# A fused two-block kernel on one core: the time-step product and seven modulation strips moved ahead, and the expert weights issued in another order

## What is computed

```python
sh_a, sc_a, g_a, sh_f, sc_f, g_f = split(silu(c) @ w_mod + b_mod, 6)     # modulation, 6 x 1024 columns
hx = x * (1 + sc_a) + sh_a ; hc = ctx * (1 + mod_c[1]) + mod_c[0]
xbc = silu(dwconv(h @ w_in[:, OFF_XBC:OFF_DT]))                          # 12 tiles of 128 channels
dt = softplus(h @ w_in[:, OFF_DT:OFF_K] + dt_bias)                       # 32 time steps per token
A = -exp(a_log) ; a_cs = cumsum(dt * A) per chunk of 128 tokens
states of the two context chunks, then y of the eight token chunks, in both directions
... gate, attention, out projection, layer norm, router ...
hid = silu(t @ w_gate[e]) * (t @ w_up[e]) ; out = hid @ w_down[e]        # two of 16 experts per token
```

## Time and profile before

| what | value |
|---|---|
| median of three runs | 3334.88 us |
| the profiled execution's own time | 3342.64 us |
| its span | 3340.5 us, so 2.1 us lie around it |
| mean granted TensorE clock | 0.952 |
| busy shares of the span | PE 92%, DVE 46%, ACT 23%, POOL 32% |
| the chain that ended last, by engine | PE 82%, DVE 7%, DMA 5%, issue 3% |

### The profile page before, as it was taken

One profiled execution on the slowest core, in us unless ns is written; L12 is line 12 of the kernel. 1 busy time (PEld: TensorE's weight loads), 2 busy tenths in 40 slices (PEclk: granted clock), 3 DMA queues, 4 the chain that ended last, 5 costly groups with the idle time before them and its releaser, 6 DMA issues.

```text
span 3340.5 us, 28822 instructions
## 1 busy us (share of the span) xinstructions
PE 3075.4 (92%) x10281; PEld 1540.7 (46%) x10281; DVE 1522.6 (46%) x2470; ACT 754.1 (23%) x1568; POOL 1059.2 (32%) x982
## 2 busy tenths in 40 slices
PE   8996999998999999999698995697899999999996
PEld 4553554444455554444444442366444444444442
DVE  2433782345666665222433223539113444544446
ACT  1223854411233333011111111512211000000002
POOL 0002770000567767100000001245004444555445
PEclk8997999999999999999799998798899999999998
DMA  6000432001000000210588887101003111121101
GB/s 256 19 0 0 118 91 92 26 26 51 1 1 1 1 1 1 67 38 29 172 302 298 322 334 277 45 0 38 26 0 101 38 38 38 38 70 44 38 13 57
DMA packets 132990, 259.53 MB, mean 78 GB/s; under 512 B 24776, under 2 KB 80752, under 8 KB 120688
## 3 DMA queue, kind: packets, MB, share of 16 engines
q1 hardware_dynamic: 120304, 216.60, 18.6%
q0 software_dynamic: 6768, 24.64, 2.1%
q10 hardware_dynamic: 5776, 16.46, 1.2%
HBM read 231.98 MB, written 25.70 MB: 77 GB/s over the span
## 4 chain that ended last, share of the span: by engine, by line
PE 82%; DVE 7%; DMA 5%; issue 3%; POOL 1%; ACT 1%; SPq 0%; ACTq 0%; DVEq 0%; POOLq 0%
PE ps L3053 16%; PE ps L3069 7%; PE ps L1453 7%; PE ps L493 6%; PE ps L1045 5%; PE ps L1857 5%; PE ps L1222 5%; PE ps L1241 4%; DMA ring<-in_w_up 4%; PE ps L1257 4%; PE ps L956 3%; PE ps L2820 3%; PE ps L1876 2%; PE ps L2122 2%; PE ps L900 1%
## 5 line engine op out<-in xcount | busy, mean ns | idle before, releaser
L1334 DVE TENSOR_REDUCE arena_b<-ps 128x1 f32<-128x512 f32 (+1 forms) x384 | 217.3, 600 | 144.4 <-PE ps L1222 144.1
L3018 POOL TENSOR_TENSOR arena_b<-arena_b,arena_d 128x512 f32<-128x512 f32 x132 | 165.7, 1271 | 370.2 <-DVE arena_d L3178 368.7
L3156 DVE TENSOR_TENSOR arena_d<-arena_d,ps 128x512 f32<-128x512 f32 x154 | 102.0, 686 | 388.1 <-PE ps L3053 388.1
L1857 PE MATMUL ps<-ring,arena_a 128*128 128x512 f32 x496 | 237.6, 635 | 33.8 <-issue 18.0
L1316 POOL TENSOR_TENSOR arena_b<-arena_b 128x512 f32<-128x512 f32 x182 | 224.5, 1267 | 92.4 <-ACT arena_b L1298 92.4
L1222 PE MATMUL ps<-arena_d,arena_a 64*128 64x512 f32 (+1 forms) x768 | 234.9, 534 | 3.6 <-DVE arena_b L1325 2.9
L1241 PE MATMUL ps<-arena_a,arena_d 64*128 64x512 f32 x640 | 220.0, 607 | 2.4 <-ACT arena_b L1298 1.8
L3175 DVE TENSOR_TENSOR arena_b<-arena_b,ps 128x512 f32<-128x512 f32 x264 | 174.8, 685 | 50.9 <-POOL arena_b L3018 25.5
L1857 PEld LDWEIGHTS ps<-ring,arena_a 128*128 128x128 f32 x496 | 99.7, 204 | 168.1 <-issue 149.5
L493 PE MATMUL ps<-arena_b,ring 128*128 128x512 f32 x384 | 166.9, 592 | 0.7 <-ACT arena_t L472 0.7
L1045 PE MATMUL ps<-ring,arena_b 128*128 128x512 f32 x384 | 167.4, 592 | 0.0
(11 more groups left out here) (546 smaller groups left out, 5363.6 us busy)
## 6 DMA issues: line engine op xcount, KB each, us to landing
ring<-in_w_gate SPq DMA_DIRECT2D x42, 1024.0 KB, 7.8
ring<-in_w_up SPq DMA_DIRECT2D x42, 1024.0 KB, 10.4
ring<-in_w_down SPq DMA_DIRECT2D x42, 1024.0 KB, 6.8
ring<-in_w_in SPq DMA_DIRECT2D x10, 2048.0 KB, 15.3
ring<-in_w_mod SPq DMA_DIRECT2D x32, 512.0 KB, 4.0
yslots<-arena_a ACTq DMA_DIRECT2D x31, 512.0 KB
ring<-in_w_mod SPq DMA_DIRECT2D x4, 2048.0 KB, 13.9
ring<-in_w_out SPq DMA_DIRECT2D x4, 2048.0 KB, 7.8
```

The lines of the kernel that those rows point to most:

```text
L1334: eng.tensor_reduce(mx3[j % 2][:, t, e, piece:piece + 1], ps[:, shared("s", u), 0:k1 - k0], AX.X, ALU.max).then_inc(s_mx, 1)
L1857: mm = eng.matmul(ps[:, s % 2, :], xsT[s % 2][:, k, :], sguw[s % 2][:, :, k, :], start=(k == 0), stop=(k == KT - 1))
```

## The change

It does four things.

1. The weight `wdtw` is transferred ahead of the first panel of `w_in`, to another place (`arena_d`).
2. The time steps are computed inside the convolution stage: the product ahead of channel tile 0, the sums behind tile 0, the chunk sums inside tile 1 (behind the first eight matmuls), DVE's part ahead of its convolution of tile 0, ACT's part behind its raw copy of tile 0. PSUM banks 3 to 7 take the results. `pe_turn(0)` waits also for DVE's copies.
3. Seven strips move: strips 0, 1 and 2 (`TAIL = 3`) stand behind the last channel tile's matmuls on TensorE, ahead of the wait for the convolution's end, and strips 3 to 6 stand in the context's steps, behind the parts hb = 1 and 3. The other 25 are spread over k = 0 to 23 as `EARLY + min(25, 25 * (k + 1) // 24)`: one in each part, two in the last. ACT's copies of strips 0 and 1 stand ahead of its last silu, that of strip 2 first in `act_ssd`, those of strips 3 to 7 in part 0.
4. In `sp_slots` gate and up of s+1 are issued ahead of down of s.

```diff
             eng.dma_start(cin, io["ctx"][0].rearrange("(t p) d -> p t d", p=P)).then_inc(s_xl[2], 16)
+            eng.dma_start(wdtw, w_in[:, OFF_DT:OFF_DT + 32].rearrange("(k p) n -> p k n", p=P)
+                                  ).then_inc(s_wdt, 16)
             load_panels(eng, J_XBC, J_XBC + 3)
             after(eng, "hx")
             eng.dma_start(hc_dram, hc.rearrange("p k n -> p (k n)")).then_inc(s_spill, 16)
-            eng.dma_start(wdtw, w_in[:, OFF_DT:OFF_DT + 32].rearrange("(k p) n -> p k n", p=P)
-                                  ).then_inc(s_wdt, 16)
...
+        TAIL, EARLY = 3, 7
+
         def strips_by(k):
-            return min(NSTRIP, (4 * (k + 1) + 2) // 3)
+            return EARLY + min(NSTRIP - EARLY, (NSTRIP - EARLY) * (k + 1) // 24)
...
         def pe_xbc(eng):
             after(eng, "hx")
+            pe_dt_product(eng)
             for m in range(XT):
...
+                if m == 1:
+                    eng.wait_ge(s_rawz, DTP_COPIED)
...
+                    if m == 1 and b == b0:
+                        pe_dt_cumulated(eng)
                 mm.then_inc(s_xbc, 1)
+                if m == 0:
+                    pe_dt_sums(eng)
                 if m >= 1:
                     pe_turn(eng, m - 1)
...
+            if m == 0:
+                eng.wait_ge(s_dt, 8)
...
+            eng.wait_ge(s_packT, DT_STEP + 1)
+            eng.tensor_copy(dtp, ps[:, 3:6, :].rearrange("p a n -> p (a n)")[:, 0:L + CTX]).then_inc(s_rawz, 1)
+            dch = Chain(eng, s_dt)
+            dve_dt(eng, dch)
             for m in range(XT):
+                if m == XT - 1:
+                    dve_condition(eng, 1)
...
             for m in range(XT + 1):
+                if m == XT:
+                    for i in range(TAIL - 1):
+                        act_strip(eng, i)
...
+                if m == 0:
+                    act_dt(eng)
...
+            act_strip(eng, TAIL - 1)
             skip(0, range(HEADS)).then_inc(s_t, 1)
...
-                for i in range(strips_by(k - 1), strips_by(k)):
+                for i in range(TAIL if k == 0 else strips_by(k - 1), strips_by(k)):
                     act_strip(eng, i)
...
-            after(eng, "dt")
+            eng.wait_ge(s_raw, XT)
+            for i in range(TAIL):
+                if i >= 1:
+                    pe_strip_sum(eng, i - 1)
+                pe_strip(eng, i)
+            after(eng, "xbc", "dt")
             cb(0)
             diff(0)
...
+                    if n < CT and hb % 2:
+                        i = TAIL + 2 * n + hb // 2
+                        pe_strip_sum(eng, i - 1)
+                        pe_strip(eng, i)
...
-            for s in range(NSLOT):
+
+            def first_weights(s):
                 e = eng.value_load(eidx[0:1, s:s + 1], min_val=0, max_val=NE - 1)
                 if s >= 2:
                     eng.wait_ge(gu_done, s - 1)
                 eng.dma_start(sguw[s % 2][:, 0], gate_of[e]).then_inc(gu_in[s % 2], 16)
                 eng.dma_start(sguw[s % 2][:, 1], up_of[e]).then_inc(gu_in[s % 2], 16)
+
+            first_weights(0)
+            for s in range(NSLOT):
+                if s + 1 < NSLOT:
+                    first_weights(s + 1)
+                e = eng.value_load(eidx[0:1, s:s + 1], min_val=0, max_val=NE - 1)
                 if s >= 2:
                     eng.wait_ge(dn_done, s - 1)
                 eng.dma_start(sdnw[s % 2], down_of[e]).then_inc(dn_in[s % 2], 16)
```

More of the change, by code:

```diff
@@ L478, in h_tile, with pe_dt_product @@
             return hx[:, k, t * P:(t + 1) * P] if t < LT else hc[:, k, (t - LT) * P:(t - LT + 1) * P]
+        dtp = view(arena_a, 6000, L + CTX)
+        DTP_COPIED = 6 + 6 + 1
+        flat = lambda v: v.rearrange("p t h -> p (t h)")
+        def pe_dt_product(eng):
+            eng.wait_ge(s_wdt, 16)
+            for b, src in enumerate((hx[:, :, 0:HALF], hx[:, :, HALF:L], hc)):
+                for k in range(KT):
+                    i = k % 4
+                    mm = eng.matmul(ps[32 * i:32 * i + 32, 3 + b, 0:src.shape[2]], wdtw[:, k, :], src[:, k, :],
+                                    start=(k < 4), stop=(k >= 4))
+            mm.then_inc(s_packT, 1)
@@ new lines, in pe_dt_sums, with pe_dt_cumulated @@
+        def pe_dt_sums(eng):
+            eng.wait_ge(s_rawz, DTP_COPIED)
+            for t in range(NT):
+                mm = eng.matmul(ps[:, 6, t * 32:(t + 1) * 32], dtp[:, t * P:(t + 1) * P], sel[:, :],
+                                start=True, stop=True)
+            mm.then_inc(s_packT, 1)
+        dt_fw, dt_bw, dt_gt = (ps[:, 6, i * NT * 16:(i + 1) * NT * 16] for i in range(3))
+        dt_all, dt_lt = ps[:, 7, 0:NT * 32], ps[:, 7, NT * 32:NT * 48]
+        def pe_dt_cumulated(eng):
+            eng.wait_ge(s_dt, 6)
+            a = dta
+            eng.matmul(dt_fw, m_le[:, :], a[:, :, 0:16], start=True, stop=True)
+            eng.matmul(dt_bw, m_ge[:, :], a[:, :, 16:32], start=True, stop=True)
+            eng.matmul(dt_all, ones[:, :], a, start=True, stop=True)
+            eng.matmul(dt_gt, m_gt[:, :], a[:, :, 0:16], start=True, stop=True)
+            eng.matmul(dt_lt, m_lt[:, :], a[:, :, 16:32], start=True, stop=True).then_inc(s_packT, 1)
@@ new lines, in act_dt @@
+        def act_dt(eng):
+            eng.wait_ge(s_dt, 2)
+            eng.wait_ge(s_small, NSMALLV)
+            eng.activation(flat(cdec), flat(eacs), ACT.Exp, scale=-1.0).then_inc(s_dta, 1)
+            eng.activation(wdt[:, 0, :], rowv("a_log"), ACT.Exp).then_inc(s_dta, 1)
+            eng.wait_ge(s_dta, 1)
+            eng.activation(flat(cdec), flat(cdec), ACT.Ln, bias=1.0).then_inc(s_dta, 1)
+            eng.wait_ge(s_dt, 8)
+            eng.activation(wdt[:, :, 0:16], dt_gt.rearrange("p (t h) -> p t h", h=16), ACT.Exp
+                           ).then_inc(s_dta, 1)
+            eng.activation(wdt[:, :, 16:32], dt_lt.rearrange("p (t h) -> p t h", h=16), ACT.Exp
+                           ).then_inc(s_dta, 1)
+            eng.activation(flat(cdec), dt_all, ACT.Exp).then_inc(s_dta, 1)
+            eng.activation(flat(eacs), flat(acs), ACT.Exp).then_inc(s_dta, 1)
@@ L540, in dve_conv @@
                 ins.then_inc(s_conv, 1)
+                if m == 0:
+                    eng.wait_ge(s_dta, 7)
+                    dch(eng.tensor_tensor(wdt, wdt, dts, ALU.mult))
             chained[0] = ch.n
@@ L3327, in _ @@
             pe_xbc(eng)
-            pe_dt(eng)
             pe_ssd(eng)
```

62 lines of the change are left out of this document (18 added, 44 removed).

## The result

The changed kernel takes 3297.1 us, the median of four runs (3294.16 to 3299.06), against 3334.24 us of four runs of the kernel before (3328.01 to 3335.53). The ratio is 0.9892, with a 95% interval of 0.9874 to 0.9909. The forecast was 3299 us, in a range of 3288 to 3315. The profiled execution took 3294.16 us, with a span of 3292.1 and a mean granted clock of 0.96.

What follows compares the result with a forecast made beforehand. TensorE bounds the kernel, busy 92% of the span; gains come where it waits or work leaves its full stretches. 20.6 - 9.2 + 8.5 - 1 + 17 = 35.9 us off gives 3299 us from the median, range 3288 to 3315.

Steps and rivals of the forecast that it cites:

- Time steps, removed: Between convolution and the context's states: the time steps alone fill the chain from 280.44 to 301.32, so 20.6 us go.
- Time steps, added: Convolution stage: product 4.8, sums 2.56 and chunk sums 1.8 us delay TensorE, together 9.2 us, or 12.1 without a clock's gain.
- Rival 5: Time steps stall the convolution and DVE ends the mixing parts: 8 us less gain, 3307 us; chance 0.12.
- The small transfer: Start of the convolution stage: moving it ahead of three panels lands them 0.5 to 1 us later, at cost 0.
- Strips out of the mixing: Mixing: seven parts lose a second strip, 7 x 1.34 = 9.4 us; 8.5 taken, 5 if DVE ends some parts.
- Strips in the tail: Convolution's end: three strips, 4.0 to 8 us, fit TensorE's 8.8 us of idling; cost 0, or 1 at low clock.
- Strips in the context's steps and the clock: Context's steps: four strips overrun DVE's gaps, cost 1 to 2 us, 1 taken; stretch left at 1.2 GHz.
- Rival 2: Context's steps: the clock comes up, a step falls from 2.93 to about 2.0 us, 7 us, 3291 us; chance 0.12.
- Expert weights: Late expert slots: weights issued 6.1 us earlier cover all late waits if transfers keep up; 17 of 18.8 us gained.
- Rival 1: Expert slots: transfers are the floor, so the slots give 0 to 5 us, total 3313 us; chance 0.13.
- The early excess: Slots 1 to 13: 30.3 us over 11.43 per slot, caused by DVE's six preparation pieces, stays as they are not touched.
- rival 4: Expert slots: weights, gathers and stores choke each other, the slots take 39 us more at 290 GB/s, 3355 us; chance 0.03.

Runs made afterwards that it cites:

- The experiment: Changed kernel with the time-step weight transferred behind the three panels of w_in, not ahead of them: 3305.66 us in a single execution.
- DVE's pieces moved: Changed kernel with the old weight order and DVE's six pieces of preparation behind modulate(s+2): 3293.79 us, 0.9871 to 0.9904 against the kernel before.
- DVE's pieces later: Changed kernel, new weight order kept, with DVE's six pieces of preparation behind modulate(s+2), ahead of the store: 3266.9 us, ratio 0.9792 against the kernel before.

## Why the prediction was right

The total was 2 us off, but by terms that miss in both directions. By its own steps:

**Time steps, removed: 20.6 forecast, 20.8 measured.** From the end of the convolution stage to POOL's first product lay 301.3 - 270.3 = 31.1 us, and now 286.8 - 276.5 = 10.3.

**Time steps, added: 9.2 forecast, 8.3 measured.** From TensorE's first matmul of the stage to its last tile's end it was 270.27 - 48.23 = 222.0 us and is 276.47 - 46.14 = 230.3. The product, the sums and the chunk sums are the 4.4, 2.2 and 1.6 us above (forecast 4.8, 2.56, 1.8). The cover of about 1 us for the turn held, with a wait of 0.24. The kernel with the time steps alone gained 13.1 us in its medians, for 11.4. Rival 5's first half (a stall in the convolution) did not come.

**The small transfer: 0, right.** The experiment shows that the product is what feels its place. That the stage starts 2.1 us sooner in the first profile after is not shown to be the change's: its first matmul starts between 47.1 and 48.3 us in the three profiles with the time steps in their old place, and between 45.5 and 48.4 in the nine with the product ahead and its weight ahead of the panels.

**Strips out of the mixing: 8.5 forecast, 5.6 measured at equal clock.** This term was mis-sized. The step that failed is "7 x 1.34": the two parts that the prediction measured were both without `cb`, and its price was carried over to all. From `diag` to `diag` at the full clock, five parts with two strips and no `cb` fell from 6.56 to 5.21 us, as forecast. Two parts with two strips and `cb` fell only from 7.00 to 6.49. Three parts with `cb` that had one strip already grew, two from 5.66 to 6.49 and one from 6.22 to 6.49. The last part with strips (k = 23), which has two now, and the part behind it cost 0.2 us more together. That adds up to 5.6. Part k = 0, the eighth with two strips, waits for DVE before and after and gives next to nothing. The chain before, behind the last row, has one of the parts of 5.66 us (398.00 - 392.34; L840 is `cb`):

```profile
392.34 1.04 PE ps L864 x8
393.37 0.50 PE ps L840 x4
...
398.00 1.03 PE ps L864 x8
```

The reason is DVE: the second strip had also been slack for it. Now each part with `cb` waits for DVE, 0.76 us for L759 beside the 0.51 of the `cb` matmuls (the chain after, at 394.79). The prediction named this and kept 5 us for it, but as the poorer case; DVE had 145 of 180 us and has two products more in a `cb` part (L720, 0.76 us). So the second half of rival 5 came in part. The two profiled executions hide it: they differ by 179.6 - 171.4 = 8.2 us, of which 2.8 are half of the 5.6 us that the first spent at 1.2 GHz.

**Strips in the tail: 0, right.** TensorE idles 4.38 us behind the third strip, ahead of `cb(0)`.

**Strips in the context's steps and the clock: a cost of 1 forecast, a gain of 4.6 between the two traces.** The step that failed is "I leave that stretch at that clock". From POOL's first product to the first `carried` it took 28.62 us and takes 23.98. The size is in part luck of the trace before: against the 24.88 us of the same old program in another execution the gain is 0.9. Rival 2 had this mechanism, at a chance of 0.12 and 7 us: a state step falls from 2.93 to 1.97 us (299.18 to 301.15), as it said, but the first 9.5 us of the stage are still at 1.2 GHz, as TensorE idles ahead of them. The trace agrees here with the Trainium skill (TensorE: Matmul & The Clock Gate, Part 1), by which the low clock is the default and activity releases it; the prediction cited it and followed the trace of another amount of work.

**Expert weights: 17 forecast, 14.1 to 18.8 measured (11.3 with DVE's pieces moved), 15.1 in the medians.** Up of slot 16 is issued at 1818.35 and wanted at 1833.56, and no late slot waits. "If the transfers keep up" was the condition: they do, at 370 GB/s and a DMA share of 0.96. The Trainium skill (DMA: Bandwidth & Descriptors, Where 436 GB/s comes from) would have made a slot 11.7 us with its 358 GB/s; the kernel sustains 370 over 154 us and, with DVE's pieces later, 364 over 27 slots, and TensorE sets the 11.43. The measurement decides against the page's figure here. Rival 1 was refuted with little to spare: as an estimate, 370 / 0.96 is 385 GB/s at the full share, 10.9 us for a slot.

**The early excess: untouched, as forecast.** Slots 1 to 13 take 178.4 us, for 178.9 and 176.2 before, and moving the pieces then takes the whole excess away. Not seen was the second cause under it: with DVE out of the way, transfers in the old order would have kept 11 us of it.

**The sum.** 20.8 - 8.3 + 5.6 + 4.6 + 16.4 = 39.1 us, for 35.9 forecast and 37.1 between the medians. The first three terms are firm to about 1 us; with 0.9 for the context's steps and 14.1 for the slots it would be 33.1. So the total was met with some luck: 2.9 us too much for the mixing and a gain that was put down as a cost take each other off, and both are smaller than the spread between executions of the kernel before (3328.01 to 3342.64 us). The two profiled executions lie 48.5 us apart, since the one before was 8.4 us above its median and the one after 2.9 below; a reader who takes the difference of the two traces for the change's effect would be 11 us off.

## What to carry to other kernels

When a wait has been put down to a transfer, look whether another engine is late by nearly as much: two causes can lie on top of each other, and taking one away may gain nothing while the other stands (here the earlier transfers alone gave 0 us, DVE's pieces alone 19, both 30, in the same 13 slots). When work leaves a stage in which TensorE never waits, what it gives back is set by the engine next in line part by part, not by that engine's mean share. And long pieces of another stage's work belong behind what TensorE waits for in a slot, not ahead of it: this was worth 30 us, nearly as much as the whole change.

## What the runs showed of the hardware

- The same program is granted different clocks in the same stretch: the mixing had no time at 1.2 GHz in one execution of the changed kernel and 8.8 us in another, and took 171.4 and 175.6 us. The context's steps took 28.62, 28.61 and 24.88 us in three executions of the same old code. An effect of less than 5 us in these stages can't be read from one pair of profiles.
- With a strip's worth of matmuls in every second gap of 0.87 us TensorE stayed at 2.4 GHz once it was there, in seven of seven executions; without it, the clock fell back in six of six.
- Weights, gathers and stores together were sustained at 364 GB/s over 308 us, with a DMA share of 0.93 to 0.95, and a weight issued ahead of time lands soon enough even there. Three streams in constant competition did not choke each other, as rival 4 had feared.
